# Routing of a two-layer MoE decoder in another order: x turned first, scores by halves, groups by match-replace

## The reference

```python
scores = sigmoid(xt @ router_w)                     # 256 x 64 experts
biased = scores + router_bias
grp_score = top_k(biased.reshape(n_tok, 8, 8), 2)[0].sum(-1)
_, top_grp = top_k(grp_score, 4)                    # 4 of 8 groups
masked = where(repeat(grp_mask, 8, axis=1), biased, -inf)
_, top_e = top_k(masked, 8)                         # 8 experts of a token
gate = scores[top_e] / sum(scores[top_e]) * 2.5
routed = segment_sum((silu(h @ w_gate[e]) * (h @ w_up[e])) @ w_down[e] * wt)
shared = (silu(xt @ sh_gate) * (xt @ sh_up)) @ sh_down
```

## Time and profile before

| | us |
|---|---|
| median of 3 runs | 1320.97 |
| lowest, highest | 1320.21, 1326.46 |
| profiled execution | 1319.62 |
| its span | 1317.9 |
| its mean granted TensorE clock | 0.972 |

### The profile page before, as it was taken

One profiled execution on the slowest core, in us unless ns is written; L12 is line 12 of the kernel. 1 busy time (PEld: TensorE's weight loads), 2 busy tenths in 40 slices (PEclk: granted clock), 3 DMA queues, 4 the chain that ended last, 5 costly groups with the idle time before them and its releaser, 6 DMA issues.

```text
span 1317.9 us, 19470 instructions
## 1 busy us (share of the span) xinstructions
PE 1213.0 (92%) x7504; PEld 723.1 (55%) x7504; DVE 576.5 (44%) x1260; ACT 373.4 (28%) x663; POOL 10.0 (1%) x30
## 2 busy tenths in 40 slices
PE   9999999998788988899999998999999788778887
PEld 8986444443344444439999997544444344334443
DVE  6656443333233223328676666734323333333224
ACT  4543222121122222125454444222222221122221
POOL 0000000000000000000000000000000000000000
PEclk9997999999899888899999999999999999999999
DMA  9966999999999999999735436699999999999994
GB/s 304 390 265 242 357 403 420 421 420 421 420 421 420 421 420 421 421 370 401 282 132 192 160 137 251 237 397 422 420 420 420 421 421 420 420 421 421 420 420 183
DMA packets 90464, 473.83 MB, mean 360 GB/s; under 512 B 8321, under 2 KB 23809, under 8 KB 42497
## 3 DMA queue, kind: packets, MB, share of 16 engines
q1 hardware_dynamic: 87440, 465.60, 87.2%
q10 hardware_dynamic: 2928, 6.94, 1.4%
HBM read 471.46 MB, written 1.05 MB: 359 GB/s over the span
## 4 chain that ended last, share of the span: by engine, by line
PE 60%; DMA 29%; SPq 5%; DVE 3%; issue 1%; ACT 1%; ACTq 0%; POOL 0%; DVEq 0%; POOLq 0%
DMA ring<-in_w_up 29%; PE ps L771 20%; PE ps L657 10%; PE ps L669 6%; PE ps L795 6%; PE ps L694 5%; SPq L456 4%; PE ps L751 3%; PE ps L833 2%; PE ps L812 2%; SPq L476 1%; PE ps L841 1%; PE ps L739 1%; PE ps L826 1%; PE ps L954 0%
## 5 line engine op out<-in xcount | busy, mean ns | idle before, releaser
L771 PE MATMUL ps<-ring,xsT 128*32 128x512 f32 (+1 forms) x2432 | 388.5, 612 | 73.9 <-DMA ring<-in_w_up 71.7
L771 PEld LDWEIGHTS ps<-ring,xsT 128*32 128x32 f32 (+1 forms) x2432 | 125.9, 124 | 325.6 <-issue 322.2
L1482 DVE SCALAR_TENSOR_TENSOR sig<-sig,slot_gate,ps 128x256 f32<-128x256 f32 x52 | 25.0, 480 | 386.5 <-ACT sig L1136 386.5
L795 PE MATMUL ps<-ring,hidT 128*32 128x512 f32 (+1 forms) x1216 | 190.1, 597 | 0.5 <-DMA ring<-in_w_down 0.3
L1279 DVE TENSOR_TENSOR ring_low<-ring,wh 128x1024 fp32r<-128x1024 f32 (+1 forms) x112 | 128.6, 1148 | 88.5 <-ACT wh L1060 87.9
L1060 ACT CAST wh<-ring 128x1024 fp32r<-128x1024 f32 (+1 forms) x112 | 110.5, 988 | 150.9 <-PE ps L657 63.7
L1136 ACT ACTIVATE sig<-ps 128x256 f32<-128x256 f32 x52 | 20.0, 384 | 430.8 <-PE ps L771 430.8
L1505 DVE TENSOR_TENSOR X<-X,ps 128x512 f32<-128x512 f32 x184 | 118.3, 682 | 52.3 <-PE ps L812 37.5
L1496 DVE TENSOR_TENSOR yl<-ps,yh 128x512 fp32r<-128x512 f32 x104 | 71.5, 691 | 124.3 <-ACT yh L1145 124.3
L1124 ACT ACTIVATE xsT<-ps,cols 128x256 f32<-128x256 f32 x208 | 102.5, 561 | 69.4 <-PE ps L751 69.4
L1145 ACT CAST yh<-ps 128x512 fp32r<-128x512 f32 x104 | 60.5, 586 | 171.8 <-PE ps L795 152.0
(11 more groups left out here) (202 smaller groups left out, 1282.8 us busy)
## 6 DMA issues: line engine op xcount, KB each, us to landing
ring<-in_w_down SPq DMA_DIRECT2D x128, 1024.0 KB, 25.3
ring<-in_w_gate SPq DMA_DIRECT2D x120, 1024.0 KB, 23.3
ring<-in_w_up SPq DMA_DIRECT2D x120, 1024.0 KB, 25.8
ring<-in_b_w_in SPq DMA_DIRECT2D x8, 3072.0 KB, 16.4
ring<-in_b_w_out SPq DMA_DIRECT2D x4, 3072.0 KB, 10.3
ring<-in_a_w_in SPq DMA_DIRECT2D x9, 1024.0 KB, 11.9
ring<-in_w_gate SPq DMA_DIRECT2D x16, 512.0 KB, 7.3
ring<-in_w_up SPq DMA_DIRECT2D x16, 512.0 KB, 8.1
```

The source lines that it names most:

```text
L771: last = nc.tensor.matmul(ps[first:first + width, p, :], xsT[:, c, p * P + first:p * P + first + width], slot_gu(slot_of(layer, k))[:, c], ...
L795: last = nc.tensor.matmul(ps[first:first + width, 4 + h, :], hidT[:, p, kk * P + first:kk * P + first + width], slot_dn(slot_of(layer, k)) ...
```

## The change

- TensorE turns both halves of x first, with two filler products ahead of the first and seven between; then the router's products follow in four groups (half 0, half 1, each in two groups of chunks). The scores of half 1 go to bank 5, and each half's scores are told by themselves (`logits` counts two).
- Only five chunks of the shared product, not seven, stand before the ranks. Chunk 5 follows the ranks, chunk 6 the keys' products, chunk 7 the first half of the first gate and up. The second pair of gathers moves behind that half, and needs only then the fourth low part. `xT0s` moves to the upper half of its place so that the lower half can be written.
- ScalarE copies the high part of half 0 first, takes the sigmoid of each half by itself, and copies the first two gathered pairs before the shared sigmoid. The loads of `sh_dn` and the two rows go from ScalarE's queue to SP's, behind the known experts' loads.
- VectorE makes the low part in four pieces in other places; bias and maxima go half by half. The groups are chosen by a maximum of eight, a match-replace and a comparison instead of by comparing all pairs. The table `tri` and its iota on GpSimd are gone, and `g_top` is set once at the start. The experts' places (`place_of`, `perm`) are now made ahead of the weights' last steps.

```diff
-        xT0s = at(xT_at, "xT0s", [P, KC, P])
+        xT0s = at(xT_at + 4 * KC * P, "xT0s", [P, KC, P])
@@ SP, behind the known experts' loads
+                sp.wait_ge(W.out_done, 2 * TT)
+                sp.dma_start(sh_dn[:], sh_down[layer].rearrange("(p c) n -> p c n", c=HC)).then_inc(g.sh_dn, 16)
+                if layer:
+                    sp.wait_ge(A.x_scaled, TT)
+                for n, dst in enumerate((gain_row, bias1_row)):
+                    sp.dma_start(dst[:], rows[4 * layer + n].unsqueeze(0).to_broadcast([P, D])).then_inc(g.rows1, 16)
                 sp.wait_ge(W.order_ready, W.past.order_ready + 1)
@@ TensorE
-                        last = nc.tensor.matmul(ps[:, 4, t * E:(t + 1) * E], (xT0s, xT1s)[t][:, c, :], rw[:, c, :],
+                        last = nc.tensor.matmul(ps[:, 4 + t, 0:E], (xT0s, xT1s)[t][:, c, :], rw[:, c, :],
...
+                keep_clock_up(3, 2)
                 transposes(0, W.x_ready, W.xT_done)
+                keep_clock_up(3, 7)
+                transposes(1, W.x_ready, W.xT_done)
                 pe.wait_ge(g.rw_in, 16 * (layer + 1))
-                router(0, range(0, 4))
-                transposes(1, W.x_ready, W.xT_done)
-                router(0, range(4, KC))
-                last = router(1, range(KC))
-                last.then_inc(W.logits, 1)
+                for t in range(TT):
+                    for half in range(2):
+                        router(t, range(4 * half, 4 * half + 4))
                 pe.wait_ge(load[s], fill_ready(layer, shared))
-                shared_gate_up(0, range(0, 7))
+                shared_gate_up(0, range(0, 5))
...
-                shared_gate_up(0, range(7, KC))
+                shared_gate_up(0, range(5, 6))
                 pe.wait_ge(W.s_ready, W.past.s_ready + 1)
-                pe.wait_ge(W.xl_ready, TT + 1)
+                pe.wait_ge(W.xl_ready, 3)
                 gather(W, 0, (0, 1))
...
-                gather(W, 0, (2, 3))
+                shared_gate_up(0, range(6, 7))
                 pe.wait_ge(W.perm_ready, W.past.perm_ready + 1)
...
                 gate_up(layer, 0, 0, range(0, 4))
+                shared_gate_up(0, range(7, KC))
+                pe.wait_ge(W.xl_ready, 4)
+                gather(W, 0, (2, 3))
@@ ScalarE: its three DMA issues and their waits are gone
+                copy_high(0, slice(0, KC))
                 act.wait_ge(g.cols_in, 16)
                 copy_xT0(0)
                 copy_xT0(1)
-                copy_high(0, slice(0, KC))
                 copy_high(1, slice(0, KC // 2))
                 copy_high(1, slice(KC // 2, KC))
-                act.wait_ge(W.logits, W.past.logits + 1)
-                nc.scalar.activation(score[:].rearrange("p a b -> p (a b)"), ps[:, 4, 0:TT * E],
-                                     ACT.Sigmoid).then_inc(W.scored, 1)
+                for t in range(TT):
+                    act.wait_ge(W.logits, W.past.logits + t + 1)
+                    nc.scalar.activation(score[:, t, :], ps[:, 4 + t, 0:E], ACT.Sigmoid).then_inc(W.scored, 1)
...
+                copy_gathered(W, 0, (0, 1))
                 shared_sigmoid(W, 0)
-                copy_gathered(W, 0, (0, 1, 2, 3))
+                copy_gathered(W, 0, (2, 3))
@@ VectorE
+                low_of_x(1, 0, first)
                 dve.wait_ge(g.cols_in, 16)
...
-                low_of_x(1, 0, slice(0, KC))
-                low_of_x(2, 1, slice(0, KC // 2))
-                dve.wait_ge(W.scored, W.past.scored + 1)
-                step(nc.vector.tensor_tensor(biased[:], score[:], rb[:, layer, :].unsqueeze(1).to_broadcast([P, TT, E]), ALU.add))
                 for t in range(TT):
+                    dve.wait_ge(W.scored, W.past.scored + t + 1)
+                    step(nc.vector.tensor_tensor(biased[:, t, :], score[:, t, :], rb[:, layer, :], ALU.add))
                     for j in range(GROUPS):
                         last = nc.vector.max(top8[:, t, j, :], biased[:, t, j * PER_GROUP:(j + 1) * PER_GROUP])
+                    if t == 0:
+                        low_of_x(1, 0, second)
...
-                step(nc.vector.tensor_tensor(g_more[:], other, own, ALU.is_gt))
-                step(nc.vector.tensor_tensor(g_tied[:], other, own, ALU.is_equal))
-                step(nc.vector.tensor_tensor(g_tied[:], g_tied[:], tri[:].unsqueeze(1).to_broadcast([P, TT, GROUPS, GROUPS]), ALU.mult))
-                step(nc.vector.tensor_tensor(g_more[:], g_more[:], g_tied[:], ALU.add))
-                step(nc.vector.reduce_sum(g_rank[:], g_more[:], AX.X))
-                step(nc.vector.tensor_scalar(g_rank[:], g_rank[:], TOPK_GROUPS - 0.5, NEG, ALU.is_gt, ALU.mult))
+                for t in range(TT):
+                    last = nc.vector.max(g_top[:, t, TOPK_GROUPS:TOPK_GROUPS + GROUPS], g_score[:, t, :])
+                step(last)
+                for t in range(TT):
+                    last = nc.vector.match_replace(g_marked[:, t, :], g_top[:, t, 0:8], g_score[:, t, :], 4 * NEG)
+                step(last)
+                step(nc.vector.tensor_scalar(g_rank[:], g_marked[:], 2 * NEG, NEG, ALU.is_gt, ALU.mult))
...
-                low_of_x(3, 1, slice(KC // 2, KC))
+                low_of_x(2, 1, first)
...
+                low_of_x(3, 1, second)
...
                 step(nc.vector.reduce_sum(w_sum[:], masked[:], AX.X))
+                dve.wait_ge(W.places, W.past.places + 1)
+                step(nc.vector.tensor_copy(place_of[:], ps[:, 1, 2 * E:2 * E + 1]))
+                nc.vector.tensor_scalar(perm[:], wanted[:], place_of[:, 0:1], None, ALU.is_equal).then_inc(W.perm_ready, 1)
                 step(nc.vector.reciprocal(w_inv[:], w_sum[:]))
```

More of the change, by code:

```diff
@@ L226, in build @@
         slot_no = sb("slot_no", [P, WIDE])
-        tri = sb("tri", [P, GROUPS, GROUPS])
+        g_top = sb("g_top", [P, TT, 4 + GROUPS])
         tie_row = sb("tie_row", [P, E])
@@ L277, in build @@
         g_score = sb("g_score", [P, TT, GROUPS])
-        g_more = sb("g_more", [P, TT, GROUPS, GROUPS])
-        g_tied = sb("g_tied", [P, TT, GROUPS, GROUPS])
+        g_marked = sb("g_marked", [P, TT, GROUPS])
         g_rank = sb("g_rank", [P, TT, GROUPS])
@@ L286, in build @@
         w_inv = sb("w_inv", [P, TT])
+        choseT = sb("choseT", [P, T])
         key_row = sb("key_row", [P, E])
@@ L291, in build @@
         perm = sb("perm", [P, 2, E])
-        choseT = sb("choseT", [P, T])
         narrow = sb("narrow", [P, E])
@@ L312, in build @@
         slot_i = sb("slot_i", [P, WIDE], I32)
-        tri_i = sb("tri_i", [P, GROUPS, GROUPS], I32)
         own_i = sb("own_i", [P, TT], I32)
@@ L348, in build @@
                        "comb_done": 8 * ROUNDS - 4, "comb_taken": 8 * (ROUNDS - 1) - 4,
-                       "logits": 1, "scored": 1, "chosen": 1, "ranks": 2, "keyed": 1, "places": 1, "perm_ready": 1,
+                       "logits": TT, "scored": TT, "chosen": 1, "ranks": 2, "keyed": 1, "places": 1, "perm_ready": 1,
                        "permuted": 1, "numbered": 1, "cols_ready": 1, "order_ready": 1, "bank45_free": 1, "over": 1,
@@ L594, in _ @@
             nc.gpsimd.iota(slot_i[:], [[1, WIDE]], base=1, channel_multiplier=0).then_inc(g.iotas, 1)
-            nc.gpsimd.iota(tri_i[:], [[1, GROUPS], [-1, GROUPS]], base=0, channel_multiplier=0).then_inc(g.iotas, 1)
             nc.gpsimd.iota(own_i[:], [[P, TT]], base=1, channel_multiplier=1).then_inc(g.iotas, 1)
@@ L825, in router @@
                     for c in chunks:
-                        last = nc.tensor.matmul(ps[:, 4, t * E:(t + 1) * E], (xT0s, xT1s)[t][:, c, :], rw[:, c, :],
+                        last = nc.tensor.matmul(ps[:, 4 + t, 0:E], (xT0s, xT1s)[t][:, c, :], rw[:, c, :],
                                                 start=(c == 0), stop=(c == KC - 1))
-                    return last
+                    if c == KC - 1:
+                        last.then_inc(W.logits, 1)
                 def shared_gate_up(t, chunks):
@@ L1513, in low_of_x @@
                                             xh[:, t, chunks].bitcast(FP32), ALU.subtract).then_inc(W.xl_ready, 1)
+                first, second = slice(0, KC // 2), slice(KC // 2, KC)
+                low_of_x(1, 0, first)
                 dve.wait_ge(g.cols_in, 16)
@@ L1522, in routing @@
                     last.then_inc(W.xT1_ready, 1)
-                low_of_x(1, 0, slice(0, KC))
-                low_of_x(2, 1, slice(0, KC // 2))
-                dve.wait_ge(W.scored, W.past.scored + 1)
-                step(nc.vector.tensor_tensor(biased[:], score[:], rb[:, layer, :].unsqueeze(1).to_broadcast([P, TT, E]), ALU.add))
                 for t in range(TT):
+                    dve.wait_ge(W.scored, W.past.scored + t + 1)
+                    step(nc.vector.tensor_tensor(biased[:, t, :], score[:, t, :], rb[:, layer, :], ALU.add))
                     for j in range(GROUPS):
                         last = nc.vector.max(top8[:, t, j, :], biased[:, t, j * PER_GROUP:(j + 1) * PER_GROUP])
+                    if t == 0:
```

(18 more changed lines are left out.)

## The result

The changed kernel takes 1310.97 us (median of 4 runs, 1310.66 to 1313.18) against 1320.91 us before (4 runs, 1320.21 to 1326.46); the ratio is 0.993 with a 95% interval of 0.9902 to 0.9958. Its profiled execution took 1310.66 us, with a span of 1308.8 us. Span against span, 9.1 us are gained.

What follows compares the result with a forecast made beforehand. TensorE was taken to bound each layer up to the second dip in the loads, the loads afterwards. Savings of 5.55 and 2.9 us, sum 8.5, take 1319.62 to 1311.1; the median, 1.35 above, is forecast at 1312, range 1307 to 1318.

Steps and rivals of the forecast that it cites:

- the second dip: Second pause of the loads, 166 to 168 us in layer 0: the layer's end moves by TensorE's shift there.
- the first refill: First load into a slot TensorE has used: starts at 125.0 instead of 133.60 us, without setting the layer's end.
- U2: Load ending the second dip, issued by SP at 166.78 us before; forecast to come near 161 us in layer 0.
- Rival (c): Loads from 134 us on: their earlier start counts in full, 1305 to 1307 us; chance 0.06.
- Rival (d): Behind the routing: late rows delay VectorE's scalings of X and eat the gain, 1315 to 1320; 0.05 with others.
- first score ready: ScalarE in the routing: copies, casts and the first score end at 109.3 us in layer 0.
- g_score to `masked`: VectorE's choice of groups: 1.1 us instead of 2.05, 0.95 us saved.
- TensorE free before the ranks: TensorE in layer 0: router and ten shared passes end at 114.4 us, before `chosen` at 115.05.
- ranks: TensorE's ranks product (L856): 115.2 instead of 122.47 us in layer 0, 831.5 instead of 836.18 in layer 1.
- GU2: Second half of the first gate and up: 128.2 instead of 133.76 us in layer 0; 2.9 us earlier in layer 1.
- short fall: TensorE's clock falls briefly after the router: 0.9 us in each layer where it happens, 1312 to 1314; chance 0.18.
- rival (a): TensorE's clock stays at the lower level from the second turning on in both layers: 1322 us; chance 0.11.

Runs made afterwards that it cites:

- part8: Changed kernel with the first refill not split but started whole after the first gate and up product; 1314.98 us, ratio to before 0.9972.
- part5: Changed kernel with the first part of the first refill taking five of eight chunks, so starting later; 1312.33 us.
- the two fillers: Changed kernel with 18 filler products, once ahead of the second dip (1319.98 us), once before the gate and up of round 6 (1311.49 us).
- split_down: Changed kernel with the last two gathers of round 1 between the two halves of unit 1's down product instead of behind it; 1309.95 us.
- no_fill_look: Changed kernel without its nine filler products, run once more for its profile; a single run of 1320.41 us.
- fill_only: Kernel before with only the nine filler products added, before and after the first turning; 1316.35 us, ratio to before 0.9968.
- act_dma: Changed kernel with the loads of sh_dn and the two rows issued by ScalarE again; 1317.79 us, ratio to before 0.9992.
- no_fill: Changed kernel without its nine filler products around the turnings; median 1318.2 us of ten runs, 1311.02 to 1323.16, one of 3039.63 left out.
- fill_turn: Changed kernel with its fillers replaced by 18 transposes of the same 128 by 128 tile; 1310.89 us.

## Why the prediction was right

*What bounds.* The claim that the end moves with TensorE at the second dip, and not with the first refill, held: 8.2 us at the refill, 5.4 us at U2, and the layer ends 5.4 us earlier (X2 at 590.10 against 595.47 us). part8, part5 and the two fillers show it by themselves. Rival (c), which counts the first refill, would have given 1305 to 1307. The claim doesn't hold exactly: in split_down half of the 1.0 us came through, in part5 0.4 and 1.3 us were lost though U2 had hardly moved. Rival (d) did not come either: the rows were issued by 104 us and landed within 19 us, and VectorE's scaling starts at 130.72 us without a wait.

*The routing's times.* Forecast and profile after, in layer 0, in us counted from X, since the mixer ended 0.42 us later this time:

| | forecast | measured |
|---|---|---|
| first score ready | 8.9 | 8.4 |
| g_score to `masked` | 1.1 | 1.11 |
| TensorE free before the ranks | 13.9 | 13.55 |
| ranks | 14.7 | 14.1 |
| GU2 | 27.7 | 27.5 |
| saved X to GU2, layers 0 and 1 | 5.5, 2.9 | 5.75, 3.15 |

The 0.5 us at the first score are mostly overlap: I had added full durations (2.1, 2.9, 2.1 and 0.28 us), while on ScalarE each instruction starts 0.1 to 0.14 us before the last one's end. Two match-replaces on eight columns take 0.38 us where I had taken 0.5 from bounds of 0.3 to 0.6. So the ranks came 0.6 us earlier than forecast in each layer. At GU2 only 0.25 us of that are left, since from the ranks to GU2 it takes 13.4 instead of the 13.0 us of the sum: a chunk of the shared product that stands by itself takes 1.05 us in the chain (L839 x2), not the 0.86 of one in a row, and two more of them now do. That GU2 fits so well is thus in part luck: two errors of opposite sign.

*The fall of the clock.* I gave it 0.11 for a long and 0.18 for a short fall, and it didn't happen. no_fill_look shows that the mechanism is real, near the price that rival (a) had: 4.1 and 5.6 us at the ranks against the 5.5 us of the forecast. Two things I hadn't seen. The gaps in front of the router's products endanger the clock as much as the missing fillers do (fill_only, act_dma). And layer 1 of the kernel before, which I took as the case with the clock up until 828.4 us, had an earlier fall too, behind the same 1.89 us of idle time as layer 0:

```profile
822.00:824.00 2.00, 2.00 (x11) 0.50 1.06 442
```

The forecast doesn't suffer, as it works from the times of the ranks and not from the clock, but more of layer 1's gain is the clock than the prediction suggests.

*The scale.* Runs of the kernel before spread from 1314.57 to 1323.44 us in 30 runs, and those of the changed kernel only from 1310.66 to 1313.18. The forecast of 1312 took the profiled execution's difference, -8.5 us, over to the median; that the median moved by 9.9 us and the profiled span by 9.1 lies within this spread. The chance of "faster" is added up wrongly by 0.01 (0.54, 0.09 and 0.06 are 0.69); nothing hangs on it. By no_fill, which spreads in the same way, the likely cause is a clock that falls in some runs and layers and not in others; for the kernel before only the falls of one execution are shown.

## What to carry to other kernels

Between a load that starts early and the end of the kernel look for the next moment in which the transfers rest: a gain counts only with what it moves there, and up to there the work and the idle time of the computing engine count, here nearly in full. Before a short, latency-bound stage is shortened, see what TensorE does meanwhile: here waits of 0.7 to 1.9 us on another engine came with a fall of the clock that put the ranks off by 2.6 to 5.6 us more, in some layers and not in others, and kernels with such waits vary more from run to run. Cheap filler products and an order without gaps belong together, as with either alone the clock fell here in one layer at least.

## What the runs showed of the hardware

- Transposes alone, 34 between the mixer's last product and the router, held TensorE's clock at the upper level as well as ordinary products did (fill_turn, 1310.89 us, clock 1.00 in both layers).
- The clock fell after idle times of 1.89 us between the two turnings (no_fill_look, both layers), of 1.52 us inside the router (fill_only, layer 1), and of 0.73 and 0.23 us before the router's first two groups (act_dma, layer 1). In layer 0 of the last two executions it stayed at 1.00 behind the same idle times, and in the changed kernel it did so behind 3.36 us before a product at 312 us. So the length of the last idle time alone doesn't tell whether it falls.
- A match-replace on eight columns costs 0.15 us beside its 0.09 us of value load, against 0.21 us on 64 columns: 56 columns more cost 0.06 us, so on eight nearly all of it is a fixed part (an estimate from these two).
